# Product stages of a two-block kernel: the low-weight matmul is issued one step after the high one

## Time and profile before

| | us |
|---|---|
| device time, median of 3 runs (lowest, highest) | 2897.41 (2896.86, 2897.66) |
| the profiled execution: span from its first to its last instruction | 2892.6 |
| the same: TensorE busy | 2737.7 (95%) |
| the same: VectorE busy, ScalarE busy | 1871.3 (65%), 1315.2 (45%) |
| the same: granted TensorE clock, mean | 0.976 |

### The profile page before, as it was taken

One profiled execution on the slowest core, in us unless ns is written; L12 is line 12 of the kernel. 1 busy time (PEld: TensorE's weight loads), 2 busy tenths in 40 slices (PEclk: granted clock), 3 DMA queues, 4 the chain that ended last, 5 costly groups with the idle time before them and its releaser, 6 DMA issues.

```text
span 2892.6 us, 44956 instructions
## 1 busy us (share of the span) xinstructions
PE 2737.7 (95%) x19186; PEld 2311.7 (80%) x19186; DVE 1871.3 (65%) x2436; ACT 1315.2 (45%) x1768; POOL 178.1 (6%) x167
## 2 busy tenths in 40 slices
PE   7999987989889899999999989999989999999997
PEld 2488876767768788888888878888878888888886
DVE  3787657777754777767866666558566556565665
ACT  1244443353334655455445555466454444343443
POOL 0121001011001000000000020000120000000001
PEclk9999998999979999999999999999999999999999
DMA  9767742232335365856766545442445555555552
GB/s 369 282 236 236 239 168 80 85 108 85 108 130 192 121 191 180 301 174 196 270 206 197 177 150 169 165 146 81 160 131 200 182 179 196 189 184 184 178 197 87
DMA packets 289207, 514.05 MB, mean 178 GB/s; under 512 B 10096, under 2 KB 122736, under 8 KB 288880
## 3 DMA queue, kind: packets, MB, share of 16 engines
q1 hardware_dynamic: 286016, 500.21, 51.7%
q0 software_dynamic: 2560, 7.90, 0.8%
q10 hardware_dynamic: 432, 3.07, 0.3%
HBM read 508.91 MB, written 2.10 MB: 177 GB/s over the span
## 4 chain that ended last, share of the span: by engine, by line
PE 85%; DVE 6%; ACT 4%; issue 3%; DMA 2%; POOL 0%; DVEq 0%; SPq 0%; ACTq 0%
PE ps L805 47%; PE ps L807 24%; PE ps L942 1%; DMA RAWa<-in_ada_w 1%; PE ps L713 1%; PE ps L773 1%; PE ps L937 1%; PE ps L927 1%; ACT WHb L1233 1%; PE ps L894 1%; PE ps L993 1%; PE ps L743 1%; DVE ACCs L1747 1%; DVE WLb L1764 1%; DVE WS L2020 1%
## 5 line engine op out<-in xcount | busy, mean ns | idle before, releaser
L805 PE MATMUL ps<-XB,WHb 128*128 128x512 f32 x2304 | 824.8, 402 | 21.7 <-issue 11.0
L807 PE MATMUL ps<-XB,WLb 128*128 128x256 f32 x2304 | 647.2, 281 | 0.0
L1764 DVE TENSOR_TENSOR WLb<-RAWb,WHb 128x2048 fp32r<-128x2048 f32 (+1 forms) x196 | 426.7, 2192 | 254.7 <-ACT WHb L1233 254.0
L805 PEld LDWEIGHTS ps<-XB,WHb 128*128 128x128 f32 x2304 | 435.7, 189 | 127.5 <-issue 19.5
L1764 DVE TENSOR_TENSOR WLd<-RAWd,WHd 128x2048 fp32r<-128x2048 f32 x144 | 328.2, 2290 | 273.6 <-ACT WHd L1233 273.6
L1233 ACT ACTIVATE WHb<-RAWb 128x2048 fp32r<-128x2048 f32 (+1 forms) x196 | 356.9, 1833 | 294.5 <-PE ps L807 260.1
L805 PE MATMUL ps<-XD,WHd 128*128 128x512 f32 x1280 | 457.5, 401 | 7.8 <-issue 6.1
L807 PEld LDWEIGHTS ps<-XB,WLb 128*128 128x128 f32 x2304 | 438.5, 190 | 0.9
L1233 ACT ACTIVATE WHd<-RAWd 128x2048 fp32r<-128x2048 f32 x144 | 274.7, 1915 | 351.6 <-PE ps L807 351.4
L805 PE MATMUL ps<-FB,WHd 128*128 128x512 f32 x1024 | 363.1, 399 | 0.0
L807 PE MATMUL ps<-XD,WLd 128*128 128x256 f32 x1280 | 360.8, 282 | 0.0
(11 more groups left out here) (334 smaller groups left out, 3564.5 us busy)
## 6 DMA issues: line engine op xcount, KB each, us to landing
RAWb<-in_ffn_w_in SPq DMA_DIRECT2D x168, 512.0 KB, 5.0
RAWd<-in_w_up SPq DMA_DIRECT2D x64, 1024.0 KB, 5.2
RAWd<-in_w_down SPq DMA_DIRECT2D x64, 1024.0 KB, 5.2
RAWa<-in_ada_w SPq DMA_DIRECT2D x48, 1024.0 KB, 7.1
RAWa<-in_rwkv_w_rkv SPq DMA_DIRECT2D x48, 1024.0 KB, 5.7
RAWb<-in_ffn_w_out SPq DMA_DIRECT2D x36, 1024.0 KB, 5.2
RAWs<-in_ada_w SPq DMA_DIRECT2D x32, 1024.0 KB, 5.0
RAWb<-in_w_in SPq DMA_DIRECT2D x44, 512.0 KB, 4.9
```

What stands on the lines that cost most here:

```text
L805: pe.matmul(bank[:, :], WH[tag][:, w, o:o + P], acts(k), start=(k == 0), stop=False)
L807: mm = pe.matmul(bank[:, 0:T], WL[tag][:, w, o:o + P], acts(k)[:, 0:T], start=False, stop=last)
L1764: dve.tensor_tensor(WL[tag][:, n % WN, 0:size], RAW[tag][:, slot, 0:size], WH[tag][:, n % WN, 0:size].bitcast(F32), ALU.subtract).then_inc ...
```

## The change

A chunk's products are listed first (`order`, in the old order), and each low matmul is held back by one step: the high matmul of the next entry is issued, then the held low. At the chunk's end the last held low is issued, so that a chunk begins with two high and ends with two low matmuls. In a k-major chunk two neighbours on the engine so never go to the same bank; in a tile-major one they still do, except where the tile changes. The waits for `s_ev` and `ready(k)` stay in front of the high matmul, the semaphore updates on the low one. The call of the hook at the chunk's middle comes after the same high matmul as before, with its low still held.

```diff
@@ -796,15 +796,19 @@
                         w, width = ch["number"] % WN, ch["width"]
                         pe.wait_ge(s_wl, ch["number"] + 1)
 
-                        def product(kk_, k, t):
+                        def high(kk_, k, t):
                             i = gm.base[g] + t
                             if k == 0 and tile_before[i] is not None:
                                 pe.wait_ge(s_ev, tile_before[i] + 1)
                             o = kk_ * width + t * P
-                            bank = banks[tile_bank[i]]
-                            pe.matmul(bank[:, :], WH[tag][:, w, o:o + P], acts(k), start=(k == 0), stop=False)
+                            pe.matmul(banks[tile_bank[i]][:, :], WH[tag][:, w, o:o + P], acts(k), start=(k == 0),
+                                      stop=False)
+
+                        def low(kk_, k, t):
+                            i = gm.base[g] + t
+                            o = kk_ * width + t * P
                             last = k == chunks[-1]["ks"][-1]
-                            mm = pe.matmul(bank[:, 0:T], WL[tag][:, w, o:o + P], acts(k)[:, 0:T],
+                            mm = pe.matmul(banks[tile_bank[i]][:, 0:T], WL[tag][:, w, o:o + P], acts(k)[:, 0:T],
                                            start=False, stop=last)
                             if last:
                                 mm.then_inc(s_tile, 1)
@@ -812,21 +816,22 @@
 
                         full = len(ch["ks"]) == 4
                         if g and ch is chunks[-1]:
-                            for t in range(nt):
-                                for kk_, k in enumerate(ch["ks"]):
-                                    mm = product(kk_, k, t)
-                                if hook and t == nt // 2 - 1 and full:
-                                    hook(g, ci, 0)
+                            order = [(kk_, k, t) for t in range(nt) for kk_, k in enumerate(ch["ks"])]
                         else:
-                            for kk_, k in enumerate(ch["ks"]):
-                                if g == 0:
-                                    if stage and k % 2:
-                                        stat(stage, k - 1, ND)
-                                    pe.wait_ge(*ready(k))
-                                for t in range(nt):
-                                    mm = product(kk_, k, t)
-                                if hook and kk_ == 1 and full:
-                                    hook(g, ci, 0)
+                            order = [(kk_, k, t) for kk_, k in enumerate(ch["ks"]) for t in range(nt)]
+                        held = None
+                        for n, (kk_, k, t) in enumerate(order):
+                            if g == 0 and t == 0:
+                                if stage and k % 2:
+                                    stat(stage, k - 1, ND)
+                                pe.wait_ge(*ready(k))
+                            high(kk_, k, t)
+                            if held:
+                                mm = low(*held)
+                            held = (kk_, k, t)
+                            if hook and n == len(order) // 2 - 1 and full:
+                                hook(g, ci, 0)
+                        mm = low(*held)
                         if ch is not chunks[-1]:
                             mm.then_inc(s_used, 1)
                         if hook:
```

## The result

| | before | after |
|---|---|---|
| device time, median (lowest to highest), us | 2897.14 (2892.78 to 2905.86), 12 runs | 2902.51 (2900.38 to 2906.10), 12 runs |
| span of the profiled execution, us | 2892.6 | 2898.5 |
| granted clock, mean | 0.976 | 0.975 |

The ratio is 1.0022, 95% interval 1.0013 to 1.003: slower, by 4 to 9 us (the two medians alone stand at 1.0019, 5.4 us apart). The forecast of 2898.7 was 3.8 us low; the range 2873 to 2910 holds the result. The profiled execution after took 2900.38 us, 1.9 more than its span. So the one before, on whose rows the prediction rests, took about 2892.6 + 1.9 = 2894.5 (an estimate), some 3 us better than its median. So both profiles show executions that were better than usual.

The account below looks back on a forecast made before the run. TensorE was taken to bound the kernel, busy 2737.7 of 2892.6 us, with the spacing of matmul starts deciding. All terms were 0 except +1.3 us for held lows, giving 2898.7 us, range 2873 to 2910.

Parts of the forecast that it names:

- rival A: In some 5,200 pairs, a matmul waits for the one before on its bank; up to 104 us faster, chance 0.12.
- Rival D: Going round the banks with every matmul lowers the granted clock in places; 176 us, 3075, chance 0.02.
- Steady stream: Inside chunks, high and low still alternate with the same operands and loads, only the banks alternate; taken at 0.
- B: The rhythm turns fast everywhere, in 2,157 to 4,000 slow pairs; 14 to 26 us faster, chance 0.12.
- C: Breaks at every chunk end hold the stream slow; 8 to 14 us lost, decisive above 900 lost fast pairs, chance 0.21.
- Chunk ends: At 388 chunks, two highs and two lows in a row replace two mixed steps; taken at 0, bound 8 us either way.
- Held lows: At 11 places waiting for a bank's release, a low is held behind the wait, 0.12 each; +1.3 us.
- Tile ends: A tile's last low comes 0.24 later for three of four tiles, delaying evacuation; taken at 0, upper bound 5 us.
- L: Rival theory in the experiments: the fast stretches before were luck, and the change has no part in it; no chance given.

Follow-up runs that it names:

- experiment 2: The changed kernel with the held low carried over chunk and group ends, so high and low alternate without that break; 2900.0 us, 1.0005 of before.
- experiment 3: The kernel before, with the change applied only from the projection on and the old order kept in the first block; 2898.70 us, 1.0002 of before.
- experiment 4: The kernel before, old order, with the raw ring and the weight rings swapped in the second block's SBUF memory; 2898.74 us, 1.0002 of before.
- experiment 5: The kernel before, with one high, high, low, low break at the 13th chunk of each of seven products; 2896.05 us, 0.9999 of before.
- experiment 6: The kernel before and the changed kernel each profiled once more without any edit; the span of before was 2886.5 us.
- twos: The order high, high, low, low all through every chunk, against the kernel before; 2878.63 us, 0.9944 of before.
- fours: Four highs, then four lows, all through every chunk, against the kernel before; 2892.86 us, 0.9995 of before.
- experiment 1: The kernel before, with only the first two pairs of each chunk issued high, high, low, low; 2900.56 us, 1.0008 of before.

## Why the prediction came out as it did

**What bounds the kernel, and rival A.** Right. The trace after has no chunk below 0.347 per pair, and experiment 2, with banks alternating in every k-major chunk, has the old lengths to a nanosecond (122.03 for 352 pairs in both). A matmul doesn't wait for the one before on its bank. The Trainium skill, "TensorE: Matmul & The Clock Gate", section "Back-to-back issue gap", gives N/2.4 + 2.5 ns for an isolated matmul and says that this over-counts at large N; a pair estimated by it is 0.325. The traces agree with neither: no steady stretch of any order tried here came below 0.3466.

**Rival D.** Fell: the clock is 1.00 in every window shown with banks alternating at every matmul.

**Steady stream, taken at 0.** This step failed, by 7.3 us in the two profiles. It asked whether the pair gets a new length, and it doesn't: the pairs had two lengths already. The prediction saw both and wrote that nothing shows which a changed order falls into; the trace of one execution indeed can't. What it missed is that the fast stretches of before aren't a property of the places. I counted them as the kernel's own, "1,158 fast pairs", with the range from there. They were one draw of several. It also took the 1814 slow pairs of the last MLP for the same rhythm, which they aren't. No order of pairs tried here made them fast, so B had less to win than it counted, and C had no support in them.

**Chunk ends, taken at 0.** Right for the break itself: 0.24 for the two lows, 0.47 for the two highs. Wrong for what follows. The bound of 8 us priced each step and not the stream behind; the 8.12 us came as 77 x 16 pairs at 0.0066. Rival C named that, with "the break at every chunk end holds the stream in the slow rhythm" and 8 to 14 us (its own sum reaches 2912, past the stated range). Its size was right against the profiled execution, in the first block, and too high against the medians (5.4). For the typical run I can only estimate. The old order has 79, 105, 44 and 33 fast chunks in four executions (before twice, experiments 3 and 4), 65 in the mean, and the change has 11 and 14: 53 x 16 x 0.0066 = 5.6 us. Its threshold of 900 lost fast pairs was passed: 77 x 16 = 1,232, less 144 won. The argument against C, that pairs behind a break were the faster ones, is answered by experiment 5: it is true behind one break and false behind the next. I should have taken such rows for single draws.

**Held lows, +1.3.** About the right size, on a wrong count. "2 + 7 + 2 = 11 places" took the entries of the earlier trace rows for waits. They are 7 places: one in `g_r`, one in the first f1 and five in the projection, at four of the seven with the matmul's idle time beside the load's. By the prediction's own price the term is 7 x 0.12 = 0.8. In the projection, where it can be read in nine traces, the held lows cost 0.9.

**Tile ends, taken at 0.** Not separated. Beyond the projection one wait grew from 0.34 to 1.10 (first f1) and one of 0.84 was new (first f2), both more than the 0.12 of reaching a wait earlier. A release that comes later by the shift of a tile's end could do that, but so can chance: the first f2's chunk with the new wait takes 6.75 after and 5.65 before, and with the old order 6.79 in experiment 3. In the second execution of the changed kernel the two waits are 0.68 and 0.25. No kernel here moved the tile ends alone.

**The sum.** +8.1 in the first block (7.3 for the rhythm, 0.8 for waits), +0.7 for the projection and `g_o2`, -1.2 in the last MLP, -1.8 for the earlier start: +5.8 of the 5.9. The forecast had the waits of the projection and none of the rhythm. That it came within 4 us is luck in part. The rhythm's 7.3 met -1.8 that the change has no part in and -1.2 that the prediction did not have, and the forecast said that nothing would be told from no change, where the interval lies clear of it.

**What stays open.** Why there are two rhythms in the first block and a third in the last MLP, and why behind a break at every chunk the first block ends in the cycle of three. Why the last MLP is never fast with pairs: in four executions with the old order there (before, experiments 4, 5 and 6) it was at 0.353, and neither the place of the weights nor the banks decides. And why twos and fours run at 0.3483 and 0.3508 in one block and at 0.3467 in the other. C as against L is settled in between: the fast stretches are drawn (experiments 3, 4 and 6), and the breaks at every chunk take them away in both executions of the change and in experiment 1. That this makes the 5.4 us of the medians is argued from the counts of single traces, as in the estimate of 5.6: experiment 1, with the same pattern, was 3.0 us above before, and its interval includes no change.

## What to carry to other kernels

Where a stream of equal instructions has two spacings in one trace, look at a second execution before you reckon with where they are: here the same program had 79 and 105 fast chunks, and whole stretches changed sides. Look at single steps too and not only at the mean: two streams at 0.353 here were not the same stream, and only one of them could turn fast as it stood. Cost a change of order not only by its steps but by what it interrupts, and try regular orders: twos gained 16 us where pairs, shifted by one, lost 5. When you count waits, count the matmul and its weight load as one. A change that takes a kernel's lucky draws away can show, as here, as a narrower spread at the worse end.

## What the runs showed that I had not expected

- **A chance state in TensorE's stream.** At a granted clock of 1.00, the same pairs of the first block take 0.3467 or 0.3533, steady over 22 chunks and more; with the old order it changes only in a product's first chunks, at the first chunk of its second group, or behind a wait or other matmuls. The 23 runs of before span 2885.43 to 2905.16, 19.7 us. The 160 sorted chunks of the first block are worth at most 160 x 16 x 0.0066 = 17 us between all fast and all slow, so part of that spread can be this; it wasn't traced run by run. It isn't all. Over the eleven traces here the first product begins at 127.1 to 131.8 us, and the stretch with the recurrence takes 434.2 to 439.3. The changed kernel's 12 runs span 5.7 us, twos' six runs 3.6.
- **An order without a draw.** High, high, low, low has no stretch at the slow rhythm in its one trace, only single chunks behind interruptions, with the same matmuls and as many weight loads.
- **Accumulating twice in a row onto one bank costs nothing.** Lows and highs on one bank next to each other and on different banks give 122.03 us for 352 pairs alike.
